# Dilated attention with three stored orders of q, and q and k loaded to 128 partitions at once

## What is computed

```python
PATTERNS = ((128, 1), (512, 4), (2048, 16))      # (window, dilation)

def _band_attn(q, k, v, win_sub, dil, rel_bias):  # on blocks of 128 rows of one residue
    ...
        s = jnp.einsum('nqhd,nkhd->nhqk', qi, ki).astype(jnp.float32) * scale + bias
        ...
        lse = jax.nn.logsumexp(s, axis=-1)
        p = jnp.exp(s - lse[..., None]).astype(vi.dtype)
        o = jnp.einsum('nhqk,nkhd->nqhd', p, vi)

def _dilated_attn_prompt(q, k, v, rel_bias):
    for w, d in PATTERNS:
        L = s // d
        o, lse = _band_attn(_to_residue(q, d), _to_residue(k, d), _to_residue(v, d), w // d, d, rel_bias)
        ...
    return _merge(outs, lses)                     # weighted by the softmax denominators
```

## Time and profile before

| | us |
|---|---|
| median of 3 runs | 2953.14 (2942.0 to 2957.29) |
| the profiled execution | 2948.5 |
| its span, first to last instruction | 2946.8 |

### The profile page before, as it was taken

The page is one execution under the profiler, slowest core; times in us unless marked ns, Lnnn a source line. Parts: engine busy times, 40 slices in busy tenths (PEclk is TensorE's granted clock), DMA queues, the critical chain, the costliest instruction groups (busy, mean ns, idle before and its releaser), DMA issues. The chain is left out here.

```text
span 2946.8 us, 43683 instructions
## 1 busy us (share of the span) xinstructions
PE 2685.3 (91%) x16598; PEld 2368.1 (80%) x16598; DVE 1241.8 (42%) x3366; ACT 884.7 (30%) x1933; POOL 888.9 (30%) x711
## 2 busy tenths in 40 slices
PE   7899999999999999996899999999934999986999
PEld 6899999999998888883799899988833777764675
DVE  3245554445000015441565556656515555543321
ACT  3312122222111111111355545545614444432000
POOL 1045454512121213211023344333441333321510
PEclk9999999999999999997999999999976999997999
DMA  4224345566232111114556666657345655535851
GB/s 156 83 74 114 103 127 154 150 184 183 67 101 90 71 57 71 44 43 122 127 117 135 148 149 139 149 115 161 89 102 158 184 183 184 181 109 192 320 181 70
DMA packets 198556, 382.27 MB, mean 130 GB/s; under 512 B 62379, under 2 KB 119955, under 8 KB 184500
## 3 DMA queue, kind: packets, MB, share of 16 engines
q1 hardware_dynamic: 156916, 229.77, 25.8%
q0 software_dynamic: 38784, 145.28, 18.7%
q10 hardware_dynamic: 2672, 4.74, 0.5%
HBM read 259.94 MB, written 125.15 MB: 131 GB/s over the span
## 5 line engine op out<-in xcount | busy, mean ns | idle before, releaser
L118 PE MATMUL bank<-w_hi,hT_hi 128*128 128x256 f32 x1792 | 508.2, 284 | 14.2 <-DMA ident<-ident 11.3
L120 PE MATMUL bank<-w_hi,hT_lo 128*128 128x256 f32 x1792 | 505.0, 282 | 0.0
L119 PE MATMUL bank<-w_lo,hT_hi 128*128 128x256 f32 x1792 | 503.6, 281 | 0.0
L1179 PE MATMUL front<-k_hi,q_st 128*128 128x256 f32 x768 | 316.5, 420 | 42.6 <-DMA k_lo<-qk 29.0
L118 PEld LDWEIGHTS bank<-w_hi,hT_hi 128*128 128x128 f32 x1792 | 339.1, 189 | 15.1 <-DMA ident<-ident 11.6
L1222 PE MATMUL obank<-turned_p,v_in 128*128 128x128 f32 (+1 forms) x1632 | 322.5, 331 | 23.8 <-ACT turned_p L1355 22.8
L120 PEld LDWEIGHTS bank<-w_hi,hT_lo 128*128 128x128 f32 x1792 | 339.5, 189 | 0.0
L119 PEld LDWEIGHTS bank<-w_lo,hT_hi 128*128 128x128 f32 x1792 | 339.0, 189 | 0.0
L1222 PEld LDWEIGHTS obank<-turned_p,v_in 128*128 128x128 f32 x1632 | 271.8, 198 | 43.0 <-ACT turned_p L1355 25.8
L1342 ACT ACTIVATE score<-score,ntop_sb 128x256 f32<-128x256 f32 (+1 forms) x768 | 289.9, 455 | 5.5 <-DMA ntop_t<-ntop 5.3
L1180 PE MATMUL front<-k_lo,q_st 128*128 128x256 f32 x768 | 274.2, 365 | 0.0
(11 more groups left out here) (299 smaller groups left out, 4980.6 us busy)
## 6 DMA issues: line engine op xcount, KB each, us to landing
qk<-xc_in SPq DMA_DIRECT2D x64, 512.0 KB, 5.1
w_raw<-w_in POOLq DMA_DIRECT2D x26, 1024.0 KB, 7.0
q_st<-qk POOLq DMA_DIRECT2D x32, 512.0 KB, 8.7
k_hi<-qk POOLq DMA_DIRECT2D x32, 512.0 KB, 11.7
k_lo<-qk POOLq DMA_DIRECT2D x32, 512.0 KB, 14.7
v_in<-v_out POOLq DMA_DIRECT2D x16, 1024.0 KB, 12.7
cum_all<-cum SPq DMA_DIRECT2D x16, 1024.0 KB, 9.8
xcT<-xc SPq DMA_DIRECT2D x12, 1024.0 KB, 3.9
```

The costliest lines, as they stand in the source:

```text
L118: pe.matmul(out, lhs_hi(k), rhs_hi(k), start=k == 0, stop=False)
L119: pe.matmul(out, lhs_hi(k), rhs_lo(k), start=False, stop=False)
L120: last = pe.matmul(out, lhs_lo(k), rhs_hi(k), start=False, stop=k == KT - 1)
L1179: pe.matmul(out, lhs, with_axes(k_hi[:, b, 0:1], axes, first), start=True, stop=False)
```

## The change

In `project`, for the 16 groups of q, a second pair of passes reads each `tables[c]` again in the order of residues modulo 4: ACT copies the high part (`take_high_by_four`) and DVE the low part (`take_low_by_four`) into one buffer `q4_parts` (the idle tile `stage`; it holds one c at a time), and SP stores it with two DMAs of 256 KB (`store_by_four`) to a new scratch tensor `q4`. The pass for c = 0 stands within `take_high(u)` and `take_low(u)`; that for c = 1 stands one or two tiles later. ACT waits until the buffer's last content is stored; PE, before it turns the next group into `tables[c]`, waits for `q4_split` too.

In `attend`, q has three tiles of one head each: `q_by1` in token order, `q_by4` by residue modulo 4 (both loaded, 1 MB each), and `q_by16`, which POOL copies out of `q_by4` (`make_q16`). The weights of all score matmuls are then 128 adjacent elements; k is read as before. k_hi and k_lo are loaded with one DMA of 1 MB each, to all 128 partitions. A head's loads are 4 DMAs of 4 MB in all, in place of 6 of 3 MB. PE waits before unit 0 of a head for `q16_made`, before unit 8 for `q4_loaded` and before unit 16 for `q_loaded`.

```diff
@@ project: names, and TensorE @@
+            q4_parts = stage[:, :, :].rearrange("p a w -> p (a w)").rearrange("p (x w) -> p x w", x=2)
+            by_four = lambda ap: ap.rearrange("p (i r) -> p r i", r=4)
+            fours = lambda ap: ap.rearrange("p (r i) -> p r i", r=4)
...
                         if u >= 1:
                             pe.wait_ge(qk_split, 2 * (u - 1) + c + 1)
+                        if 1 <= u <= QK_GROUPS // 2:
+                            pe.wait_ge(q4_split, 2 * (u - 1) + c + 1)
@@ project: ScalarE @@
                         act.copy(qk_parts[:, 0, c, :].bitcast(F32R), tables[c][:, :]).then_inc(qk_high, 1)
+                        if c == 0 and u < QK_GROUPS // 2:
+                            take_high_by_four(u, c)
+
+                def take_high_by_four(u, c):
+                    if 2 * u + c >= 1:
+                        act.wait_ge(q4_stored, 32 * (2 * u + c))
+                    if c == 1:
+                        act.wait_ge(qk_split, 2 * u + 2)
+                    act.copy(fours(q4_parts[:, 0, :].bitcast(F32R)), by_four(tables[c][:, :])).then_inc(q4_high, 1)
...
+                    if n % RING == 0 and 1 <= n // RING - 1 <= QK_GROUPS // 2:
+                        take_high_by_four(n // RING - 2, 1)
@@ project: VectorE @@
+                        if c == 0 and u < QK_GROUPS // 2:
+                            take_low_by_four(u, c)
+
+                def take_low_by_four(u, c):
+                    dve.wait_ge(q4_high, 2 * u + c + 1)
+                    dve.tensor_tensor(fours(q4_parts[:, 1, :].bitcast(F32R)), by_four(tables[c][:, :]), fours(q4_parts[:, 0, :]),
+                                      ALU.subtract).then_inc(q4_split, 1)
...
+                    if n % RING == 1 and 1 <= n // RING - 1 <= QK_GROUPS // 2:
+                        take_low_by_four(n // RING - 2, 1)
@@ project: SyncE @@
+                def store_by_four(u, c):
+                    slab, quad = u // 4, u % 4
+                    sp.wait_ge(q4_split, 2 * u + c + 1)
+                    for x in range(2):
+                        dst = bass.AP(tensor=scr["q4"].tensor, offset=(x * D + slab * SLAB + c * P) * SEQ + P * quad,
+                                      ap=[[SEQ, P], [512, 4], [1, P]])
+                        sp.dma_start(dst, fours(q4_parts[:, x, :])).then_inc(q4_stored, 16)
@@ attend: tiles @@
-        q_st = sb("q_st", [P, 2, SEQ], F32R)
+        q_by = {p: sb(f"q_by{d}", [P, SEQ], F32R) for p, d in enumerate(DILATIONS)}
@@ attend: GpSimd @@
-            def load_qk(h):
-                if h >= 2:
-                    pool.wait_ge(front_ready, scores_end[h - 2])
-                for half in range(2):
-                    rows = slice(half * HD, (half + 1) * HD)
-                    for dst, x in ((q_st, half), (k_hi, 2), (k_lo, 3)):
-                        pool.dma_start(dst[rows, h % 2, :].bitcast(F32), scr["qk"][x, h * HD:(h + 1) * HD, :]).then_inc(qk_loaded[h % 2], 16)
+            def load_k(h):
+                if h >= 2:
+                    pool.wait_ge(front_ready, scores_end[h - 2])
+                for dst, x in ((k_hi, 2), (k_lo, 3)):
+                    pool.dma_start(dst[:, h % 2, :].bitcast(F32), head_rows(x, h, 0)).then_inc(k_loaded[h % 2], 16)
+            def load_q(h):
+                if h >= 1:
+                    pool.wait_ge(front_ready, scores_end[h - 1])
+                pool.dma_start(q_by[0][:, :].bitcast(F32), head_rows(0, h, D * SEQ)).then_inc(q_loaded, 16)
+            def load_q4(h):
+                if h >= 1:
+                    pool.wait_ge(q16_made, h)
+                    pool.wait_ge(front_ready, unit_done(h - 1, 2 * UNITS // 3 - 1))
+                pool.dma_start(q_by[1][:, :].bitcast(F32), head_rows(0, h, D * SEQ, "q4")).then_inc(q4_loaded, 16)
+            def make_q16(h):
+                pool.wait_ge(q4_loaded, 16 * (h + 1))
+                if h >= 1:
+                    pool.wait_ge(front_ready, unit_done(h - 1, UNITS // 3 - 1))
+                pool.tensor_copy(q_by[2][:, :].rearrange("p (m r j) -> p m r j", m=4, r=4),
+                                 q_by[1][:, :].bitcast(F32).rearrange("p (r j m) -> p m r j", r=4, m=4)).then_inc(q16_made, 1)
+                pool.wait_ge(q16_made, h + 1)
...
                 if h % 2 == 1 and h + 1 < H:
                     pool.wait_ge(mixed, NG * h + 12)
                     load_v(pool, 1, (h + 1) // 2)
+                if h + 3 < H:
+                    load_q4(h + 3)
                 if h >= 1:
                     normalise(h - 1, (h - 1) % 2)
+                if h + 3 < H:
+                    make_q16(h + 3)
@@ attend: TensorE @@
                 if 0 in units:
-                    pe.wait_ge(qk_loaded[b], 96 * (h // 2 + 1))
+                    pe.wait_ge(k_loaded[b], 32 * (h // 2 + 1))
+                    pe.wait_ge(q16_made, h + 1)
+                if UNITS // 3 in units:
+                    pe.wait_ge(q4_loaded, 16 * (h + 1))
+                if 2 * UNITS // 3 in units:
+                    pe.wait_ge(q_loaded, 16 * (h + 1))
...
-                        lhs = with_axes(q_st[:, b, 0:1], [[d, P]], P * d * blk + r)
+                        q_at = (P * blk, 4 * P * r + P * blk, P * r)[p]
+                        lhs = q_by[p][:, q_at:q_at + P]
```

More of the change, by code:

```diff
@@ L365, in project @@
             qk_stored = [sem(f"qk_stored{c}") for c in range(2)]
+            q4_high, q4_split, q4_stored = sem("q4_high"), sem("q4_split"), sem("q4_stored")
             mhalf_set = sem("mhalf4_set")
@@ L724, in store_qk @@
                         sp.dma_start(dst, qk_parts[:, :, c, :]).then_inc(qk_stored[c], 16)
+                        if c == 0 and u < QK_GROUPS // 2:
+                            store_by_four(u, c)
+                def store_by_four(u, c):
[5 more added lines that the diff above has]
+                        sp.dma_start(dst, fours(q4_parts[:, x, :])).then_inc(q4_stored, 16)
                 for s in range(QK_SLABS):
@@ L734, in _ @@
                             store_qk(n // RING - 1)
+                        if t % RING == 1 and 1 <= n // RING - 1 <= QK_GROUPS // 2:
+                            store_by_four(n // RING - 2, 1)
                     sample_store(s, 0)
@@ L941, in attend @@
         const_in = sem("const_in")
-        qk_loaded = [sem(f"qk_loaded{b}") for b in range(2)]
+        k_loaded = [sem(f"k_loaded{b}") for b in range(2)]
+        q_loaded, q4_loaded, q16_made = sem("q_loaded"), sem("q4_loaded"), sem("q16_made")
         v_loaded = [sem(f"v_loaded{p}") for p in range(3)]
@@ L1098, in _, with head_rows, unit_done @@
         def _(pool):
-            def load_qk(h):
+            def head_rows(x, h, apart, of="qk"):
+                first = scr[of][x, h * HD:(h + 1) * HD, :]
+                return bass.AP(tensor=first.tensor, offset=first.offset, ap=[[SEQ, HD], [apart, 2], [1, SEQ]])
+            def unit_done(h, u):
+                return place["score", h, u] + 1
+            def load_k(h):
                 if h >= 2:
                     pool.wait_ge(front_ready, scores_end[h - 2])
-                for half in range(2):
-                    rows = slice(half * HD, (half + 1) * HD)
-                    for dst, x in ((q_st, half), (k_hi, 2), (k_lo, 3)):
-                        pool.dma_start(dst[rows, h % 2, :].bitcast(F32), scr["qk"][x, h * HD:(h + 1) * HD, :]).then_inc(qk_loaded[h % 2], 16)
+                for dst, x in ((k_hi, 2), (k_lo, 3)):
[16 more added lines that the diff above has]
+                pool.wait_ge(q16_made, h + 1)
             def apply_gate(h, b, pair):
@@ L1122, in normalise @@
                 pool.wait_ge(finished, h + 1)
-            for h in range(2):
-                load_qk(h)
+            load_q4(0)
+            load_k(0)
+            load_q(0)
+            load_k(1)
+            make_q16(0)
             pool.memset(v_in[:, :, 0:HD - 1], 0.0).then_inc(ones_set, 1)
@@ L1130, in _ @@
             pool.wait_ge(ones_set, 4)
-            for p in (2, 1, 0):
+            load_q4(1)
+            make_q16(1)
+            load_v(pool, 2, 0)
+            load_q(1)
+            for p in (1, 0):
                 load_v(pool, p, 0)
-            load_qk(2)
+            load_k(2)
+            load_q4(2)
+            make_q16(2)
             for h in range(H):
@@ L1141, in _ @@
                     pool.wait_ge(ntop_loaded, 32 * (h + 2))
-                    load_qk(h + 3)
+                if h + 2 < H:
+                    load_q(h + 2)
+                if h + 3 < H:
+                    load_k(h + 3)
                 if h % 2 == 1 and h + 1 < H:
@@ L2451 @@
     "qk": (4, D, SEQ),
+    "q4": (2, D, SEQ),
     "z": (SEQ, D),
```

4 lines of the change are left out of this document (added).

## The result

The changed kernel takes 3009.02 us (median of 4 runs, 3002.86 to 3015.62), the kernel before 2951.41 us beside it: a ratio of 1.020, 95% interval 1.017 to 1.023. In the profiled execution the span grew from 2946.8 to 3003.1 us, by 56.3.

| stretch | before | after | change | forecast |
|---|---|---|---|---|
| start to G(0) | 1393.5 | 1450.3 | +56.8 | +66 |
| G(0) to G(3) | 101.3 | 105.8 | +4.5 | +12 |
| G(3) to G(15) | 569.6 | 569.8 | +0.2 | +130 |
| G(15) to the end | 882.4 | 877.1 | -5.3 | 0 |

A forecast was written before the change was run, and what follows sets the result against it. PE was taken to set the pace in the q slabs and to be busy 96% in the heads, where nothing at a head's start waits for the chain. 66 + 12 + 140 - 10 = +208 on 2953: about 3160 us, range 3050 to 3245.

The forecast's parts named there:

- The q slabs: q projection: copies, subtractions and stores through the one q4 buffer loop in 17.4 us a group against PE's 13.0; +66 us.
- Score matmuls: Attention scores: k's gap holds PE, so adjacent q weights save only 0.1 us per unit ahead of `meet`; -10 us.
- the rival of the weights: Score matmuls: gapped weight loads bound PE, so dilations 16 and 4 lose 0.1 us a matmul; 3117 us, chance 0.10.
- Start of the attention: First heads: head 2's copy comes late, its load queued behind v's 3 MB; +12 us, 4 to 20.
- The copy: POOL's copy of 128 x 2048 from `q_by4` to `q_by16` takes 4.0 us a head, 2.0 to 8.0.
- The dear copy: Rival on POOL's copy: reading every fourth element takes twice as long, 8.0 us; 3208 us, chance 0.12.
- The heads: Heads 3 to 15: PE waits for POOL's copy behind `normalise`, a loop of 59.2 us a head; +140 us.
- The other edits cost nothing: Remaining edits: few SP stores in the q slabs, k's loads hidden as before, POOL idle 355 us; no cost.
- The chain's length: Heads: from the start of a head's scores to the end of `normalise`, 52.4 heavy, 45.9 light, mean 49.2 us.
- the surcharges: Added to each head's loop: 4 us for `q_by4`'s load beside the reciprocals' read-back (0 to 6), 2 for PE's clock.
- The clock: Heads: PE idles some 10 us before each head and starts at 1.2 GHz; 2 us a head, 0 to 3.5.
- The chain eases: Rival on the heads: no more contention, no clock loss, a copy of 2 us, 96 us less; 3064 us, chance 0.12.

## Why the prediction was wrong

- **The q slabs: right.** Forecast loop 17.4 us, +66; measured 16.7, +57 at G(0). The landings were 4.8 and 4.2 against 5.5 and 4.5, the engine steps 4.4 and 3.0 against 4.1 and 2.9. Two buffers give all of it back.
- **Score matmuls: right in the result, half right in the reason.** In after they start 0.22 us apart at dilation 16 (rows below, timeline of PE behind G(6)) and 0.23 at dilation 4, though a load there now lasts 0.21 us in the median. The step read "the matmul waited for the moving operand of the one before", so k's gap holds PE. It does, but so does q's: with k adjacent the steps stay where they are. The row on which I rested could not tell: its next load was adjacent, so it showed only that k's gap suffices. Of the rival of the weights this leaves a half that I had not written down.

```profile
1704.01 0.40 PE L1270 MATMUL front<-k_hi,q_by 128*128 128x256 f32 x1
1704.23 0.40 PE L1271 MATMUL front<-k_lo,q_by 128*128 128x256 f32 x1
```

- **Start of the attention: the wrong wait.** +12 forecast, +4.5 to G(3). The copy for head 2, which was to be 12 us late, cost PE 2.3 us. PE stood 13.7 us before head 1 instead, for `q_by1`: the scores of heads 0 and 1 are made in one go and wait for all three tiles of q ahead of their first unit. Of this 8.9 us came back, a wait for DVE that stood in head 1 before.
- **The copy:** 4.0 forecast, 3.8 to 3.9 measured. The dear copy falls. It takes no longer than the pass over adjacent elements of the earlier trace rows, but that pass adds a second input; no run has a copy of adjacent elements on POOL, so what the gap costs, if anything, stays open.
- **The heads: the failed step.** 59.2 us a turn, measured 47.5. The 11.7 us can be split by the run with halves of 64 partitions. In it a turn is 53.5, so 6.0 come from where the loads go: "The other edits cost nothing" counted k's loads as hidden, which they are, but not what they do to the 8 KB write beside them, which let the read-back go after 11.3 us before and after 6.5 now. The chain's length was taken from a trace in which this write had slow loads beside it, and the change made these loads fast. The other 5.7 are the surcharges: +4 for contention with `q_by4`'s load and +2 for the clock. In that run both are at work, and the chain is 49.6 long, not 49.2 + 6. In the changed kernel the stretch from the read-back to `normalise` is 7.8 us in the mean where it was 7.1, so 0.7 of the +4 showed.
- **The clock:** PE does start a head slower, 0.89 in the 15.2 us after G(6), but over the heads the mean is 0.97 before and after.
- **The rivals.** "The chain eases" (3064 us) had the right direction but took off only 96 us, where the heads alone were 130 too dear. The range could not reach the result: even with every surcharge at its least a turn was to be 51.2 us, since the chain's 49.2 had no bound of its own, and it was this term that measured 43.5.

## What to carry to other kernels

When a change alters DMAs that nobody waits for, look at who shares the engines with them: here an 8 KB write on the longest chain moved, from 11.3 to 6.5 us, and a chain's length taken from the old trace was only as good as the old traffic. Load to partitions spread over both halves of SBUF, even in two DMAs, and keep the dimension of the partitions outermost. When two inputs of an instruction have a gap, a test of one says nothing of the other: take away both before judging either.

## What was unexpected of the hardware

- Loads of 512 KB to 64 partitions, all in one half of SBUF, bring POOL's queue to 69 engine-us a MB, and on every other partition to 48 (606 and 352 ns for a packet of 8 KB); an 8 KB write beside them lets its read-back go after 11.1 to 11.5 us against 5.3 to 6.7.
- Of three 1 MB loads with a dimension of 2 outermost in their source the last landed after 39.6 us in place of 9.3.
- A gap in weights or in the moving operand puts score matmuls of 256 columns 0.22 to 0.24 us apart, either alone; both together put them no further apart, and only without either is it 0.12.
